# A new SBUF map: the area with the squared activations moves down, the weights move up

## The reference

```python
def _sq_relu_mlp(h, w1, w2):
    a = jax.nn.relu(h @ w1)          # (512, 1024) @ (1024, 4096)
    return (a * a) @ w2              # (512, 4096) @ (4096, 1024)

for i in range(DEPTH):               # DEPTH = 2
    h, gate = _modulate(x, c, norm_g[i, 0], ada_w[i, 0], ada_b[i, 0])
    y = _ab_mixer(h, ...) if i % 2 == 0 else _cd_mixer(h, ...)
    x = x + gate * y
    h, gate = _modulate(x, c, norm_g[i, 1], ada_w[i, 1], ada_b[i, 1])
    x = x + gate * _sq_relu_mlp(h, mlp_w1[i], mlp_w2[i])
return _rmsnorm(x, final_g)
```

## The kernel before

| | before |
|---|---|
| h_hi, h_lo | 16,384 and 32,768 |
| w_raw (2) | 49,152 |
| w_hi (2), w_lo (2) | 65,536 and 81,920 |
| modulation rows, constants, work tiles | 98,304 to 127,871 (ones at 111,104) |
| shared area | 127,872 |
| a_hi, a_lo in it | 127,872 and 144,256 |
| toep, yg in it | 163,200 and 179,584 |

## Time and profile before

### The profile page before, as it was taken

The page is one execution under the profiler, slowest core; times in us unless marked ns, Lnnn a source line. Parts: engine busy times, 40 slices in busy tenths (PEclk is TensorE's granted clock), DMA queues, the critical chain, the costliest instruction groups (busy, mean ns, idle before and its releaser), DMA issues.

```text
span 1247.1 us, 15894 instructions
## 1 busy us (share of the span) xinstructions
PE 1222.3 (98%) x6200; PEld 990.8 (79%) x6200; DVE 747.1 (60%) x1029; ACT 506.1 (41%) x700; POOL 82.6 (7%) x122
## 2 busy tenths in 40 slices
PE   6999999999999999999999999999999999999998
PEld 4789888888888888888788875568888888888887
DVE  8999987674554455486688948756833332333332
ACT  5543436514314314325432258861651441432431
POOL 0010000000000000140000001215000000000032
PEclk9999999999999999999999999999999999999999
DMA  9558791844443453422232220003233233332221
GB/s 327 190 135 244 279 331 60 291 133 171 177 159 136 177 177 133 164 76 90 79 102 87 83 69 1 1 1 102 68 129 91 84 101 101 101 101 75 93 67 68
DMA packets 132699, 157.59 MB, mean 126 GB/s; under 512 B 19784, under 2 KB 113152, under 8 KB 132608
## 3 DMA queue, kind: packets, MB, share of 16 engines
q1 hardware_dynamic: 125328, 153.82, 36.9%
q10 hardware_dynamic: 7312, 2.96, 1.0%
HBM read 151.39 MB, written 4.19 MB: 125 GB/s over the span
## 4 chain that ended last, share of the span: by engine, by line
PE 93%; ACT 2%; DMA 2%; DVE 2%; issue 1%; ACTq 0%
PE psum L1806 92%; PE psum L1810 2%; DMA ada_first<-in_ada_w 1%; ACT pT L1111 1%; DMA raw_bn<-in_ssm_b_im 1%; DVE work L1390 1%; DVE h_lo L1430 0%; DVE w_lo L1376 0%; ACT h_hi L855 0%; ACT xT L800 0%; ACTq L948 0%; ACT w_hi L786 0%; DVE work L1421 0%; ACT sp_sb L1064 0%; ACT rstd L848 0%
## 5 line engine op out<-in xcount | busy, mean ns | idle before, releaser
L1806 PE MATMUL psum<-h_hi,w_hi 128*128 128x512 f32 (+1 forms) x872 | 343.0, 393 | 1.1 <-DVE w_lo L1376 1.1
L1806 PE MATMUL psum<-h_lo,w_hi 128*128 128x512 f32 (+1 forms) x872 | 339.6, 389 | 0.0
L1806 PE MATMUL psum<-h_hi,w_lo 128*128 128x512 f32 (+1 forms) x872 | 339.5, 389 | 0.0
L786 ACT ACTIVATE w_hi<-w_raw 128x2048 fp32r<-128x2048 f32 x92 | 174.4, 1895 | 285.6 <-PE psum L1806 285.1
L1376 DVE TENSOR_TENSOR w_lo<-w_raw,w_hi 128x2048 fp32r<-128x2048 f32 x92 | 212.9, 2314 | 88.5 <-ACT w_hi L786 87.9
L1806 PE MATMUL psum<-a_hi,w_hi 128*128 128x512 f32 x512 | 202.5, 396 | 0.0
L1806 PE MATMUL psum<-a_hi,w_lo 128*128 128x512 f32 x512 | 202.1, 395 | 0.0
L1806 PE MATMUL psum<-a_lo,w_hi 128*128 128x512 f32 x512 | 202.1, 395 | 0.0
L1806 PEld LDWEIGHTS psum<-h_hi,w_hi 128*128 128x128 f32 (+1 forms) x872 | 163.5, 188 | 39.1 <-issue 3.6
L1806 PEld LDWEIGHTS psum<-h_hi,w_lo 128*128 128x128 f32 (+1 forms) x872 | 163.3, 187 | 34.7
L1806 PEld LDWEIGHTS psum<-h_lo,w_hi 128*128 128x128 f32 (+1 forms) x872 | 163.5, 188 | 33.2
(11 more groups left out here) (318 smaller groups left out, 1346.2 us busy)
## 6 DMA issues: line engine op xcount, KB each, us to landing
w_raw<-in_mlp_w SPq DMA_DIRECT2D x64, 1024.0 KB, 5.3
ada_l_ring<-in_ada_w SPq DMA_DIRECT2D x64, 384.0 KB, 5.9
w_raw<-in_cd_w_in SPq DMA_DIRECT2D x14, 1024.0 KB, 5.2
ada_ring<-in_ada_w SPq DMA_DIRECT2D x17, 384.0 KB, 6.0
ada_more<-in_ada_w SPq DMA_DIRECT2D x15, 384.0 KB, 4.6
ada_first<-in_ada_w SPq DMA_DIRECT2D x5, 1024.0 KB, 14.8
w_raw<-in_ab_w_in SPq DMA_DIRECT2D x4, 1024.0 KB, 7.4
w_raw<-in_ab_w_out SPq DMA_DIRECT2D x4, 1024.0 KB, 8.2
```

What stands on the lines that cost most here:

```text
L786: act.activation(w_hi[n % 2][:, :, 0:w], raw[n % 2][:, :, 0:w], ACT.Copy).then_inc(hi_ready, 1)
L1806: return nc.tensor.matmul(o, lhsT, rhs, start=start, stop=stop, **kw)
```

## The change

The shared area gets a fixed length (`ARENA`, 84,800 bytes) and its place right behind `h_lo`. The raw weights, split weights, modulation rows, constants and work tiles follow above it, each in the same order as before and each moved up by 84,800 bytes. Inside the area nothing moves. Only this is in the diff:

```diff
+ARENA = 32 * 2650
...
     h_hi = place("h_hi", [P, KC, L], F32R)
     h_lo = place("h_lo", [P, KC, L], F32R)
+    arena = cursor[0]
+    arena_end = arena + ARENA
+    cursor[0] = arena_end
     raw = [place(f"w_raw{i}", [P, 8, SLOT]) for i in range(2)]
     w_at = cursor[0]
...
     pool_w_t = place("pool_w_t", [P, 4, P])
-    arena = cursor[0]
-    assert arena - sumsq_at >= 4 * 10 * P
+    assert cursor[0] <= nc.sbuf_usable_end, (cursor[0], nc.sbuf_usable_end)
+    assert cursor[0] - sumsq_at >= 4 * 10 * P
...
-    assert at[0] <= nc.sbuf_usable_end, (at[0], nc.sbuf_usable_end)
+    assert at[0] <= arena_end, (at[0], arena_end)
```

## The result

The changed kernel takes 1279.06 us (median of four executions, 1269.26 to 1285.74) against 1253.37 us before on the same chip: ratio 1.0196, 95% interval 1.0144 to 1.0248. Timed once more in another set it was 1284.38 us against 1251.86, ratio 1.0246 (1.0192 to 1.0300). It is 1.4 to 3.0% slower, above the top of my range.

What follows compares the result with a forecast made beforehand. TensorE's matmul spacing was taken to bound the kernel. Terms -5.1 - 4.5 - 0.3 + 2.5 = -7.4 us took 1255.06 to 1247.7 us, range 1242 to 1277.

Steps and rivals of the forecast that it cites:

- the bound's 17.1: Products over h with weights moved high: the other bound, each h product at a's spacing, 2,592 x 6.6 = 17.1 us lost.
- Moving operands up to byte 98,303 have the short spacing: All float32r groups: the moving operand's place sets the spacing, 6.6 ns per matmul in layer 1; chance 0.42, 1247.7 us.
- First change, a: MLP products over a, moved to bytes 49,152 to 81,919: 5.1 us gained in layer 1 and 4.5 in layer 0.
- Second, yg: The GLU's 48 products over yg, moved to bytes 100,864 to 117,247: 0 to 0.3 us gained, 0.3 taken.
- Third, the weights as stationary operand: Weights moved to bytes 150,336 to 183,103, stationary for h and a: 0 taken by load times, up to 17.1 us lost.
- Fourth, VD and VC: VD and VC, with the weights as moving operand now high: 384 x 6.6, 0 to 2.5 us lost, 2.5 taken.
- The low-bit rival: Float32r products: low address bits of the operands set the spacing; 1185 us at best, 1299 at worst; chance 0.11.
- The place has nothing to do with it: Products over a: spacing comes from something unnamed in that stage and stays; no change, 1255.1 us; chance 0.14.
- Distance: Float32r products: operands on different sides of a point between bytes 98,304 and 127,872 cost 6.6 ns; +19.6, 1274.7 us; chance 0.33.
- The Trainium skill's rule that I weighed: TensorE's SBUF reads: independent ports, no place dearer than another; sum 0, 1255.1 us; given a small chance only.
- No wait is added: Whole kernel: instructions, semaphores, DMAs and their queue order stay as they are, and no step moves past another.
- the rest hangs behind TensorE: VectorE, ScalarE and slot loads: 4.2 of 10.9 us leave over 6 us of cover per weight slot; 0 cost.

Runs made afterwards that it cites:

- Experiment 1: Separate matmul-only kernel: 36 float32r products per pair of low or high places, moving tile shifted by 64 bytes; at 512 columns 8.20 us at offset 0, 8.41 us at 192.
- experiment 8: Separate matmul-only kernel: finer operand offsets, other column counts, plain float32 and bfloat16; float32r with 512 columns 226.7 ns at offset 0, 236.7 at 4 bytes.
- experiment 11: Kernel before with 64 unused bytes ahead of toep, so toep, u_run and yg move up: 1258.21 us against 1252.49, ratio 1.0048.
- experiments 9 and 10: mods moved to the front of the map: in the kernel before (1246.84 us, ratio 0.9959); in the changed kernel, with ARENA = 32 * 2640 (1246.88 us, ratio 0.9967).

## Why the prediction was wrong

**What held.** TensorE's spacing bounds the kernel, and VectorE and ScalarE kept their times. The question, too, was the right one. In the rows of before, 6.6 ns of each a product depend on where its operands lie, and 2,592 h products would pay for it if they came to the same state. They did: 16.0 us against the bound's 17.1.

**The step that failed first** is the one from the groups to the place. "Moving operands up to byte 98,303 have the short spacing [...], those from 127,872 on the long one" fits every row of before, but so does the offset. Every moving operand that was low there was also at offset 0 and every high one at 128. I held the offset as the rival with the smallest chance, since four groups fell so neatly into low and high; four groups with only two distinct offsets could not tell these apart. Experiment 1 shows that place is nothing with 512 columns: 8.20 us at offset 0 in all four combinations of low and high.

**By terms of the sum.** *First change, a:* -9.6 forecast, +0.7 measured; the offset went from 128 to 192, and both are dear. *Second, yg:* -0.3 forecast, 0 measured, for the same reason. *Third, the weights as stationary operand:* 0 forecast, +16.0 measured. "I take 0, by the load rows" is the step that carries most of the miss in the matmuls, 16.0 of the 23.2 us between the -7.4 forecast and the +15.8 measured; a's 9.6 that didn't come is next. The loads took 188 ns before and 188 to 189 after, so the load rows could not see this cost; and the float32 rows that I took as support could not either, since float32 has 429.2 ns at every offset (experiment 8). I had written that float32 may hide what float32r shows, and should have kept to that. *Fourth, VD and VC:* +2.5 forecast, -0.9 measured: 120.0 to 117.8 ns inside the groups, from offset 0 to 64, and at 256 columns 64 is cheaper than 0. "Goes with each matmul and not with its columns" is wrong; the order of the offsets depends on the number of columns.

**The low-bit rival** had the mechanism, and its time was left open between 1185 and 1299. Its condition was half right. The offset counts modulo 256, not 512, and h and a did come to share one spacing, which is close to a's own; but "all 4,560 products share one spacing" left out that the sign and the number of columns count, and VD and VC went the other way. With a's spacing for h that sum would have been 17.1 - 0.9 + 0.7, about 1272 us. *The place has nothing to do with it* fell with the first row of the profile after: the h products changed with nothing but their tiles' places. *Distance* gave 1274.7, near the truth by luck, by a mechanism that experiment 1 refutes: a time that comes out right proves no mechanism. The Trainium skill's rule that I weighed ("SBUF — State Buffer", section "Who interferes with whom": independent read ports for moving operand and weight loads, TensorE never waits on another engine) is no guide here either. It speaks of engines; experiment 1 has nothing but matmuls, at most 2 GB/s of DMA traffic in the stretches shown and no other engine at work, and its spacing changes by 3% with the two operands' addresses modulo 256. Whether the ports have a part in that no run here shows.

**The part that I did not see.** "No wait is added" and "the rest hangs behind TensorE" are the other steps that failed. They were checked for the parts of the weights and for the slot loads, and not for copies whose rows are 64 to 512 bytes long. From the first issue of toep to its use there are 10.7 us in the kernel before, and the last row lands 0.1 us ahead of the use: after, the same way took 12.7 us, and TensorE waits for 1.5 of the 1.9 more. I named no cover for them, and there was next to none. Off their multiple of 512 the two sets of copies cost 1.9 to 5.0 us of waits in eight profiles. "DMA: Bandwidth & Descriptors", of the Trainium skill, says in its section "Specifications" that a transfer needs 512 bytes to run at line rate. That concerns the size of a row; here rows of one size differ by up to 1.9 times (448 bytes, 33 and 62 ns) with the place of their tile, and rows of 512 bytes, which have the page's size, differ too (36 ns before, 66 in experiment 11).

Behind the wait the clock falls, and that is nearly as dear as the rest: 12.5 us in the profiled execution. By the mean clock it comes in six of ten of the changed kernel's executions, against 12 of 54 of before. The chain is shown in parts. Shown is that with the tiles from toep on moved, and nothing else, the waits appear (experiment 11), and that with both kept on a multiple of 512 they don't (experiments 9 and 10, in either order of the map). Over all kernels with the two tiles off it, 35 of 50 executions have a mean clock under 0.99, over those with the tiles on it 15 of 73. Not shown is that the wait is what triggers the fall. In favour is the table: the fall comes in the seven profiles with the longer waits and in none of the other four. Against it, experiment 11 has longer waits than the changed kernel with fewer low means (5 of 12), and 12 of 54 executions of before have them without the copies off their place. Why the offset of two operands changes the spacing stays open as well: the runs give values, not a mechanism. So does whether the copies ask for a multiple of 512 bytes or only of 256. No kernel had the tiles 256 past a multiple of 512; but the rows of u_run are 256 bytes long and lie one behind another, so half of them stand there in every kernel, the quick ones too.

The account, then: h +16.0, VD and VC -0.9, a +0.7, waits for copies +2 to +4, one more short fall of the clock +1.6, the rest +1, which makes some 20 us where the clock has no long fall, and 12.5 (the profile) to 16 us (the medians of the two groups of executions) more where it has. The median of ten executions falls among the latter. Without the long fall the time (1268.7 to 1274.3) lies inside my range, held there by the bound of 17.1 for h; what carried it above is a term that the sum did not have.

## What to carry to other kernels

In a kernel bound by float32r matmuls of 512 columns, put the moving and the stationary tiles on the same address modulo 256 bytes and measure that before anything else about the map; a 384-byte tile in the wrong place cost this one 0.4%, and 64 bytes of padding in the wrong place, with the late copies and the lower clock that came with them, cost 2.4%. Put the tiles that small DMA rows write on multiples of 512 bytes, and look at how long before its use each of them lands. When products get faster, look at which engine's result is now late: here GpSimd's was, by 0.7 us, and the clock fell behind it. When a grouping of the rows suggests a cause, list what else the groups share, address bits included, and give the rival that the rows can't exclude its own time.

## What the runs showed of the hardware

The spacing of float32r products of 128x128 weights and 512 columns goes by the moving minus the stationary address, modulo 256 bytes: 226.7 ns at 0, 228.9 at 64, 232.3 at 128, 233.3 at 192, 236.7 at 4 bytes; with 256 columns 120.0, 117.8 and 118.8 at the first three, and 113.3 or 117.8 at 192. Neither plain float32 nor bfloat16 shows it. Packets of 256 bytes took 24 to 27 ns into a tile that starts on a multiple of 512 and 32 to 45 into one that starts 64, 128 or 448 past one. In seven of eleven profiles of the whole kernel the granted clock fell to 0.50 for 27.3 or 30.7 us between 105 and 141 us from the start, behind a wait of 1.5 to 2.3 us for toep, with TensorE busy throughout the stretch at the lower level. And with a at 226.7 ns a wait of 0.7 us for GpSimd, which no profile with a at 232.4 to 233.3 ns has, came with a fall of 3.4 us.
